# Six of eight embedding products made between the layer norm's turns and gates, and copied out of PSUM by ScalarE

## The reference, cut to what matters

```
y = (mixer output) @ w_out
x = layer_norm(ALPHA * x + y, ln_g[i], ln_b[i])
x = x + (p[i] @ ple_w[i]) * jax.nn.sigmoid(x @ ple_gate_w[i])
```

## Time and profile before

| | us |
|---|---|
| median of 3 runs | 1772.87 (1770.1 to 1775.2) |
| the profiled execution, its own time | 1763.42 |
| its span in the trace | 1761.7 |
| PE busy | 1608.7 (91% of the span) |
| DVE / ACT / POOL busy | 720.7 / 519.5 / 593.6 |
| mean granted TensorE clock | 0.919 of full speed |

### The profile page before, as it was taken

How to read it: one execution, slowest core, us unless ns; L and a number is a source line. 1 busy time by engine, 2 the same in 40 slices (tenths; PEclk the granted TensorE clock), 3 DMA queues, 4 the chain that set the end, 5 groups by cost and what they waited for, 6 DMA issues and landing times. The chain is left out here.

```text
span 1761.7 us, 23121 instructions
## 1 busy us (share of the span) xinstructions
PE 1608.7 (91%) x9729; PEld 1341.3 (76%) x9729; DVE 720.7 (41%) x1479; ACT 519.5 (29%) x841; POOL 593.6 (34%) x247
## 2 busy tenths in 40 slices
PE   6998999999989988989897998999999877959899
PEld 6896876999979765866675997897887643649889
DVE  4031430331163635977665125312301555586331
ACT  2443224331123123243343112342221235211211
POOL 5333420433333263534642333332442360500213
PEclk8999999999999988999998999999999786578869
DMA  4313220225223220320111422242222000000102
GB/s 147 90 57 94 72 72 1 75 94 179 96 72 97 77 79 24 96 72 24 49 48 32 173 73 84 96 128 78 91 95 72 1 0 1 0 30 1 64 26 98
DMA packets 116721, 121.58 MB, mean 69 GB/s; under 512 B 14607, under 2 KB 110841, under 8 KB 116362
## 3 DMA queue, kind: packets, MB, share of 16 engines
q1 hardware_dynamic: 113072, 114.16, 20.6%
q10 hardware_dynamic: 3546, 5.94, 0.9%
HBM read 113.80 MB, written 6.29 MB: 68 GB/s over the span
## 5 line engine op out<-in xcount | busy, mean ns | idle before, releaser
L175 POOL TENSOR_TENSOR w_low<-w_ring,w_high 128x2048 fp32r<-128x2048 f32 (+2 forms) x95 | 422.5, 4448 | 896.9 <-ACT w_high L166 896.8
L191 PE MATMUL ps<-w_high,xT_high 128*128 128x256 f32 (+1 forms) x1056 | 305.9, 290 | 9.9 <-issue 6.9
L191 PE MATMUL ps<-w_high,xT_low 128*128 128x256 f32 (+1 forms) x1056 | 300.9, 285 | 0.0
L191 PE MATMUL ps<-w_low,xT_high 128*128 128x256 f32 (+1 forms) x1056 | 300.9, 285 | 0.0
L166 ACT ACTIVATE w_high<-w_ring 128x2048 fp32r<-128x2048 f32 (+2 forms) x95 | 174.1, 1833 | 362.4 <-PE ps L191 349.7
L191 PE MATMUL ps<-xT_high,w_high 128*128 128x512 f32 (+3 forms) x624 | 255.4, 409 | 8.7 <-DVE mix_a L724 7.7
L191 PE MATMUL ps<-xT_low,w_high 128*128 128x512 f32 (+3 forms) x624 | 250.8, 402 | 0.0
L191 PE MATMUL ps<-xT_high,w_low 128*128 128x512 f32 (+3 forms) x624 | 249.4, 400 | 0.0
L191 PEld LDWEIGHTS ps<-w_high,xT_high 128*128 128x128 f32 x1056 | 204.8, 194 | 15.2 <-issue 14.9
L191 PEld LDWEIGHTS ps<-w_low,xT_high 128*128 128x128 f32 x1056 | 204.8, 194 | 1.3 <-issue 1.2
L191 PEld LDWEIGHTS ps<-w_high,xT_low 128*128 128x128 f32 x1056 | 204.2, 193 | 0.0
(11 more groups left out here) (500 smaller groups left out, 2416.3 us busy)
## 6 DMA issues: line engine op xcount, KB each, us to landing
w_ring<-in_gla_w_in_dram SPq DMA_DIRECT2D x24, 1024.0 KB, 5.4
w_ring<-in_dsa_w_in_dram SPq DMA_DIRECT2D x19, 1024.0 KB, 5.2
w_ring<-in_w_in_dram SPq DMA_DIRECT2D x18, 1024.0 KB, 5.1
w_ring<-in_gla_w_out_dram SPq DMA_DIRECT2D x8, 1024.0 KB, 5.2
w_ring<-in_ple_gate_w_dram SPq DMA_DIRECT2D x8, 1024.0 KB, 5.0
w_ring<-in_dsa_w_out_dram SPq DMA_DIRECT2D x8, 1024.0 KB, 5.0
w_ring<-in_w_out_dram SPq DMA_DIRECT2D x8, 640.0 KB, 4.3
x_scratch<-x SPq DMA_DIRECT2D x4, 1024.0 KB, 6.9
```

What stands on the lines that cost most here:

```text
L175: self.nc.gpsimd.tensor_tensor(self.w_low[:, i % RING, 0:k, 0:cols], self.w_ring[:, n % RING, 0:k, 0:cols], self.w_high[:, i % RING, 0:k, ...
L191: return self.nc.tensor.matmul(out, lhs, rhs, start=first, stop=last, skip_group_check=not check)
```

## The change

In each output stage, six of the eight embedding products, (n, j) = (0,0) to (0,3), (1,0) and (1,1), are made early and one at a time. They are called E0 to E5 here. E0 stands behind T1, E1 behind G0 and ahead of T2, E2 behind T2, E3 behind G1 and ahead of T3, E4 behind T3, and E5 behind G2. They use the banks that the gate pieces of j = 1, 2, 3 will write: E0 and E1 bank 5, E2 and E3 bank 6, E4 and E5 bank 7. ACT copies each into a new SBUF buffer `ple` (`copy_embedded`, semaphore `ple_copied`), which lies over a part of the mixer output that is no longer needed. So the odd ones wait for the copy of the one before, and the gate piece of tile j waits for `ple_copied` 2j. DVE multiplies these six from SBUF, not from PSUM. The embedding block between the halves vanishes for n = 0, and has two products left, (1,2) and (1,3), for n = 1. On ACT, `high(2)` now stands ahead of `deviation(3)`.

```diff
+        early_ple = [(0, 0), (0, 1), (0, 2), (0, 3), (1, 0), (1, 1)]
+        ple_bank = lambda u: NT + 1 + u // 2
+        ple = g.alias(f"ple{layer}", [P, len(early_ple), COLS], F32, gT_at + 4 * NT * D)
...
+                def embed(bank, n, j):
+                    for k in range(KP):
+                        ins = g.product(ps[:, bank, :], pT[:, k, j * P:(j + 1) * P], w_ple[:, k, n * COLS:(n + 1) * COLS], k == 0, k == KP - 1)
+                    return ins
+
+                def embed_early(u):
+                    if u % 2 == 0:
+                        pe.wait_ge(sem["y_added"], past["y_added"] + NT + ple_bank(u) - NT + 1)
+                    else:
+                        pe.wait_ge(sem["ple_copied"], past["ple_copied"] + u)
+                    embed(ple_bank(u), *early_ple[u]).then_inc(sem["ple_early"], add("ple_early", 1))
+
+                embed_early(0)
...
+                                if j:
+                                    pe.wait_ge(sem["ple_copied"], past["ple_copied"] + 2 * j)
...
-                            if half == 0 and n == 0 and j < 2:
-                                normed(j + 2)
+                            if half == 0 and n == 0 and j == 0:
+                                embed_early(1)
+                                normed(2)
+                                embed_early(2)
+                            elif half == 0 and n == 0 and j == 1:
+                                embed_early(3)
+                                normed(3)
+                                embed_early(4)
+                            elif half == 0 and n == 0 and j == 2:
+                                embed_early(5)
...
                         if half == 0:
                             for j in range(NT):
-                                tile = slice(j * P, (j + 1) * P)
-                                for k in range(KP):
-                                    ins = g.product(ps[:, j, :], pT[:, k, tile], w_ple[:, k, n * COLS:(n + 1) * COLS], k == 0, k == KP - 1)
-                                ins.then_inc(sem["ple_ready"], add("ple_ready", 1))
+                                if (n, j) not in early_ple:
+                                    embed(j, n, j).then_inc(sem["ple_ready"], add("ple_ready", 1))
...
+                def copy_embedded(u):
+                    act.wait_ge(sem["ple_early"], past["ple_early"] + u + 1)
+                    nc.scalar.activation(ple[:, u, :], ps[:, ple_bank(u), :], ACT.Copy).then_inc(sem["ple_copied"], add("ple_copied", 1))
+
                 high(0)
                 g.split_high(act, gates + 1)
                 high(1)
+                copy_embedded(0)
                 deviation(2)
                 g.split_high(act, gates + 2)
+                copy_embedded(1)
+                high(2)
+                copy_embedded(2)
                 deviation(3)
-                high(2)
+                copy_embedded(3)
                 high(3)
+                copy_embedded(4)
+                copy_embedded(5)
...
-                    dve.wait_ge(sem["ple_ready"], past["ple_ready"] + i + 1)
-                    nc.vector.tensor_tensor(gate[:, i % 2, :], gate[:, i % 2, :], ps[:, j, :], ALU.mult).then_inc(sem["ple_gated"], add("ple_gated", 1))
+                    if (n, j) in early_ple:
+                        u = early_ple.index((n, j))
+                        dve.wait_ge(sem["ple_copied"], past["ple_copied"] + u + 1)
+                        embedded = ple[:, u, :]
+                    else:
+                        dve.wait_ge(sem["ple_ready"], past["ple_ready"] + i - len(early_ple) + 1)
+                        embedded = ps[:, j, :]
+                    nc.vector.tensor_tensor(gate[:, i % 2, :], gate[:, i % 2, :], embedded, ALU.mult).then_inc(sem["ple_gated"], add("ple_gated", 1))
```

## The result

The changed kernel takes 1756.91 us (median of 6, 1751.76 to 1763.14) against 1771.48 us before (6 runs, 1763.38 to 1775.2). The measured ratio is 0.9931, 95% interval [0.9902, 0.9961], so 12.2 us faster, between 7 and 17; the two medians themselves lie 14.6 us apart. The forecast was 1763.3 us in [1757.5, 1770.5], a gain of 9.6 us. The direction is right, and the 9.6 us lie in the measured interval. The median itself lies 0.6 us under the forecast's range; on the base that the forecast used, 1772.87 x 0.9931 = 1760.6 us, it lies inside.

A forecast was written before the change was run, and what follows sets the result against it. PE's work, its holes and its stretches at the lower clock bound the kernel. Gains of 1.3 + 3.45 + 1.4 + 3.45 = 9.6 us took 1772.9 to 1763.3 us, range 1757.5 to 1770.5.

The forecast's parts named there:

- PE's work does not change; gain comes from holes and clock: Output stage: 10.3 us of products per layer come back elsewhere; gain only from filled holes and a clock staying up.
- the two holes: PE idle before G0, 3.44 us, and before T2, 2.03 us in layer 0 and 3.53 us in layer 1.
- POOL first, by 0.2 us: Second gate chunk: POOL's subtraction starts about 0.2 us ahead of DVE's tile 2 instruction, so T2 stays at 503.16 us.
- The bound of 2.05 us a layer: Ahead of T2: gain of 0 if POOL is first, 2.05 us a layer if DVE is (chance 0.22).
- T2 to half 1 in 18.1 us, with one wait: PE from T2 to half 1: 18.1 us, 0.9 us of it waiting for E5's copy; gain 1.3 and 1.4 us.
- n = 1, 3.45 us: Embedding block between the halves of n = 1: two products fewer, 3.45 us gained in each layer.
- The held multiplication costs nothing: First DVE multiplication of n = 0 from SBUF: held 2.6 us by POOL, cover 4 us, so no cost.
- The clock rival: Around the holes the clock falls anyway: gain 6.2 us, 1766.7 us, or 2.8 us, 1770 us; chance 0.22.
- the forecast's step of carrying the difference between two profiled executions over to the median unchanged: Whole kernel: the 9.6 us gain taken off the profiled 1763.4 us was also taken off the median 1772.9 us.

The follow-up runs named there:

- E5: Early embedding product (1,1), behind G2; the changed kernel without it, product back in the block of n = 1: 1759.67 us, 0.9934 of before.
- the wait on POOL: POOL's second gate chunk subtraction waits for normed(2): added to the changed kernel, 0.9928 of before; added to the kernel before, 0.9975.
- after again: The changed kernel measured once more, unchanged: 1755.56 us, 0.9922 of before.
- the kernel with four products: Against the changed kernel: four early products, two between T1 and G0, two between G1 and T3; both POOL waits; `deviation(3)` ahead of E2's copy: 1744.13 us, 0.9855 of before.

## Why the prediction was right, step by step

- **PE's work does not change; gain comes from holes and clock.** Right: 1611.3 against 1608.7 us busy, with the two holes filled by 1.72 us each and the clock at 1.00.
- **POOL first, by 0.2 us.** Right at 0.21 us in both layers, and L1106 held in every trace without the wait on POOL. The bound of 2.05 us a layer was measured with that wait: T2 comes 2.05 and 2.01 us earlier behind T1, and the stages are 2.24 and 2.02 us shorter. The rule of the Trainium skill, "SBUF — State Buffer", "Who interferes with whom", that whichever issues first holds the other for its whole instruction, agrees with the rows of L1106: 1.28 us first and 5.40 to 5.42 us second. At the scaling of tile 3 the starts that the traces show do not settle who issued first.
- **T2 to half 1 in 18.1 us, with one wait.** Right: 506.12 to 524.33 us, 18.2. The wait was in it with 0.9 and is 0.94.
- **n = 1, 3.45 us.** The mis-sized term, in layer 0. The embedding block shrank as said, but half 1 of n = 0 and half 0 of n = 1 ran at a slower pace than before, 0.5 us over 192 matmuls (23.04 against 22.51 us). Hence 4.16 and not 4.75 us there; layer 1, with 4.71 for 4.85, is nearly exact.
- **The held multiplication costs nothing.** Right: 3.24 us, 2.6 more than alone, with no wait on PE.
- **The clock rival.** Did not come in any of the seven traces with early products: 1.00 from T1 to half 1 in both layers. By what the Trainium skill says of turns ("TensorE: Matmul & The Clock Gate", Part 4), that they do not count as PE being busy in the same way, the clock might have fallen at T2. No trace with early products shows it fall there, and no run tests the rule.
- **What the working did not see.** That G1 at half speed hid a third hole, ahead of T3, of 1.3 us. The sum was right, because E2 and E3 stood there; the reason behind it, that only E0 and E1 lay in holes, was wrong, and that the sum came out in spite of it is luck. Nor did it see that the change would move the race at the scaling of tile 3, which costs 3 to 4 us in an execution in which POOL wins. It took the profiled execution to gain the 9.6 us too, at 1753.8; it took 1763.14.
- **The size of the whole.** 12.2 us [7, 17] measured, and 13.8 [9.6, 17.9] in the repeat, against 8.9 in the stages. What the other 3 to 5 us are stays open. The same kernel against itself was 2.6 us apart, and in the traces outside the stages the shifts go both ways by 1 to 3 us. The granted clocks of whole executions say more: the 11 runs of before beside the repeat have a median of 0.913, where the profiled execution of before has 0.919; the six of the repeat of after have 0.923, where its profiled one has 0.921. So executions of before mostly lose more clock than the one that was profiled. Where they lose it, no trace shows, and the forecast's step of carrying the difference between two profiled executions over to the median unchanged is not borne out. Part may also be the scaling of tile 3, if DVE is held there in executions of before without a profile; that was not shown.

## What to carry to other kernels

Work that depends on nothing gains only where it fills a hole; list the holes as they will be once the clock is up, since a slow stretch hides the next one, and lay the pieces by that list, each with a bank that makes nobody wait. Four of the products placed in this way, with POOL kept behind two DVE instructions, gained 25.7 us where six without those waits gained 12 to 14. When two engines exclude each other, who comes first may hang on a tenth of a microsecond; no kernel here came out measurably slower by a semaphore that orders them, and it takes the chance out.

## What was not expected of the hardware

**A scaled tile held by 0.04 us.** DVE's instruction is shown as started 0.04, 0.02 and 0.03 us ahead of POOL's in after, after again and after without E5, and was yet the one held. With 0.16 or 0.17 us in hand, in the two traces of before and the two in which only the wait for normed(2) was added, and with 0.39 us with two early products, it went first. What decides lies between, a little behind the start that the trace shows.

**Three paces of the same matmul at the full clock.** By their starts, 256-column matmuls in a long row follow each other at 0.117, 0.119 or 0.120 us, and keep the pace that they have until the row ends. Ten microseconds each, PE busy throughout, all at a clock of 1.00. Behind a block of four products: before in layer 0, before in layer 1, and before with the wait on POOL in layer 0:

```profile
524.00:534.00 10.00, 10.00 (x88) 10.00 (x87) 4.14 (x6) 1.79 (x3) 0.00 (x0) 1.00 0.31 102
1090.00:1100.00 10.00, 10.00 (x87) 10.00 (x86) 4.14 (x6) 3.33 (x8) 0.00 (x0) 1.00 0.26 91
518.00:528.00 10.00, 10.00 (x85) 10.00 (x85) 4.14 (x6) 1.80 (x3) 0.00 (x0) 1.00 0.33 104
```

Behind the single E5 and its wait: after, and after with POOL waiting for normed(2), both in layer 0:

```profile
525.00:535.00 10.00, 10.00 (x85) 10.00 (x85) 6.39 (x6) 4.59 (x5) 4.62 (x1) 1.00 0.27 83
525.00:535.00 10.00, 10.00 (x87) 10.00 (x86) 7.91 (x8) 3.60 (x4) 2.79 (x2) 1.00 0.34 107
```

In the kernel with four products, behind two products and the turns T3:

```profile
506.00:516.00 10.00, 10.00 (x88) 10.00 (x87) 1.93 (x3) 4.13 (x4) 2.68 (x1) 1.00 0.01 3
```

Over 192 matmuls the paces lie up to 0.5 us apart, as much as the forecast missed in layer 0. All three stand behind a block of four, and two of them behind the same wait, so what stands ahead of the row does not settle the pace. What does, no run shows.
